# Two-layer decoder trunk on one core: both heads of a pair on the two halves of the array

## The reference, cut to what matters

```python
scores = jnp.einsum('bdnqhc,bdnkhc->bdnhqk', qs, kk) * (hd ** -0.5)
scores = jnp.where(allowed[:, None], scores + bias, NEG_INF)
m = jnp.max(scores, axis=-1)
p = jnp.exp(scores - m[..., None])
l = jnp.sum(p, axis=-1)
o = jnp.einsum('bdnhqk,bdnkhc->bdnqhc', p, vv.astype(jnp.float32))
...
cross = cross_attention(qc, mem_n, w_mem_kv[i])
x = x + jnp.concatenate([mix, cross], axis=-1) @ w_out[i]
```

## Time and profile before

| | us |
|---|---|
| median of 3 runs | 1661.31 |
| the profiled execution | 1662.92 |
| its span | 1661.1 |
| TensorE busy (PE) | 1584.7 (95%) |
| VectorE busy (DVE) | 1306.5 (79%) |
| ScalarE busy (ACT) | 1117.8 (67%) |
| GpSimd busy (POOL) | 79.8 (5%) |

### The profile page before, as it was taken

How to read it: one execution, slowest core, us unless ns; L and a number is a source line. 1 busy time by engine, 2 the same in 40 slices (tenths; PEclk the granted TensorE clock), 3 DMA queues, 4 the chain that set the end, 5 groups by cost and what they waited for, 6 DMA issues and landing times.

```text
span 1661.1 us, 25537 instructions
## 1 busy us (share of the span) xinstructions
PE 1584.7 (95%) x8450; PEld 1341.2 (81%) x8450; DVE 1306.5 (79%) x1687; ACT 1117.8 (67%) x1442; POOL 79.8 (5%) x57
## 2 busy tenths in 40 slices
PE   7899988999988989799999999999999999999996
PEld 6899966999987766688888888888888888888885
DVE  4777755555557763799899899899899899999996
ACT  5554445434443653687887878888878878878874
POOL 1422100000000000000000000000000000000000
PEclk9999988999998998799999999999999999999998
DMA  9744425566632235599999999999999999999992
GB/s 263 196 126 119 135 64 149 158 187 181 186 84 66 81 129 189 182 401 387 367 398 386 356 389 382 374 385 376 382 384 367 390 383 367 391 385 354 403 387 77
DMA packets 226976, 455.34 MB, mean 274 GB/s; under 512 B 12832, under 2 KB 120496, under 8 KB 226928
## 3 DMA queue, kind: packets, MB, share of 16 engines
q1 hardware_dynamic: 222784, 439.52, 72.9%
q0 software_dynamic: 4144, 15.22, 3.7%
HBM read 445.52 MB, written 9.18 MB: 274 GB/s over the span
## 4 chain that ended last, share of the span: by engine, by line
PE 90%; DVE 5%; ACT 2%; DMA 2%; issue 1%; DVEq 0%; POOL 0%; ACTq 0%; POOLq 0%
PE ps L664 27%; PE ps L665 26%; PE ps L666 26%; PE ps L737 2%; DMA big<-in_even_w_in 2%; PE ps L1029 1%; DVE w_lo L1345 1%; PE ps L759 1%; PE ps L735 1%; PE ps L746 1%; ACT w_hi L1065 1%; PE ps L691 1%; PE ps L763 0%; PE ps L971 0%; PE ps L962 0%
## 5 line engine op out<-in xcount | busy, mean ns | idle before, releaser
L1345 DVE TENSOR_TENSOR w_lo<-big,w_hi 128x1024 fp32r<-128x1024 f32 (+1 forms) x843 | 992.4, 1218 | 233.8 <-ACT w_hi L1065 157.0
L1286 ACT CAST w_hi<-big 128x1024 fp32r<-128x1024 f32 x672 | 693.8, 1056 | 138.0 <-PE ps L666 134.0
L664 PE MATMUL ps<-w_hi,m_hi 128*128 128x512 f32 (+1 forms) x1008 | 393.7, 391 | 4.6 <-DVE w_lo L1345 4.6
L665 PE MATMUL ps<-w_lo,m_hi 128*128 128x512 f32 (+1 forms) x1008 | 391.0, 388 | 0.0
L666 PE MATMUL ps<-w_hi,m_lo 128*128 128x512 f32 (+1 forms) x1008 | 390.6, 388 | 0.0
L664 PE MATMUL ps<-h_hi,w_hi 128*128 128x256 f32 (+1 forms) x824 | 240.5, 292 | 5.0 <-DVE w_lo L1345 5.0
L665 PE MATMUL ps<-h_lo,w_hi 128*128 128x256 f32 (+1 forms) x824 | 236.2, 287 | 0.0
L666 PE MATMUL ps<-h_hi,w_lo 128*128 128x256 f32 (+1 forms) x824 | 235.9, 286 | 0.0
L1065 ACT CAST w_hi<-big 128x1024 fp32r<-128x1024 f32 (+1 forms) x171 | 165.3, 977 | 95.5 <-PE ps L666 82.7
L664 PEld LDWEIGHTS ps<-w_hi,m_hi 128*128 128x128 f32 x1008 | 190.6, 189 | 44.7 <-issue 7.2
L666 PEld LDWEIGHTS ps<-w_hi,m_lo 128*128 128x128 f32 x1008 | 190.6, 189 | 38.7
(11 more groups left out here) (218 smaller groups left out, 1320.4 us busy)
## 6 DMA issues: line engine op xcount, KB each, us to landing
big<-in_odd_w_gate SPq DMA_DIRECT2D x112, 1024.0 KB, 7.3
big<-in_odd_w_up SPq DMA_DIRECT2D x112, 1024.0 KB, 7.5
big<-in_odd_w_down SPq DMA_DIRECT2D x112, 1024.0 KB, 7.4
big<-in_even_w_in SPq DMA_DIRECT2D x42, 512.0 KB, 4.2
big<-in_even_w_gate SPq DMA_DIRECT2D x22, 512.0 KB, 3.9
big<-in_even_w_up SPq DMA_DIRECT2D x22, 512.0 KB, 3.8
big<-in_even_w_down SPq DMA_DIRECT2D x22, 512.0 KB, 3.5
big<-in_w_out SPq DMA_DIRECT2D x20, 512.0 KB, 4.4
```

The source lines that it names most:

```text
L664: mm(dst, a[0], b[0], start=start, stop=False, **kw)
L665: mm(dst, a[0], b[1], start=False, stop=False, **kw)
L1286: nc.scalar.copy(w_hi[:, slot, :], ring[s][:, (u % 2) * UNIT:(u % 2 + 1) * UNIT]).then_inc(s_hi, 1)
L1345: return V.tensor_tensor(dst, src, lead.bitcast(F32), ALU.subtract)
```

## The change

The two heads of a pair now go through the scores together: `scores` issues their matmuls in turn, one on rows 0 to 63, one on rows 64 to 127, each into a bank of its own. `mix` does the same with the two column halves. For this the second head has buffers of its own: banks 1 and 7 and the second half of a projection bank for its scores (the third window's, of both heads), `zq` (where the indexer's queries and keys also live) for its scaled scores in layer 0, half of pr for its probabilities, `selm` or `zq` for their transpose. The orders of TensorE, ScalarE and VectorE in a step follow. Two semaphores are new: `third_left` (the first head's third window is written, before the second's is) and `third_read` (the next projection may take the bank). GpSimd's masks of a pair wait for the probabilities of both heads of the pair two before.

```diff
@@ buffers @@
-        qiT = sb("qiT", [P, 4, SEQ])
-        kiT = sb("kiT", [P, SEQ])
+        zq = sb("zq", [P, 5 * SEQ])
+        qiT = zq[:, 0:4 * SEQ].rearrange("p (c n) -> p c n", c=4)
+        kiT = zq[:, 4 * SEQ:5 * SEQ]
@@ views @@
-            return (z[:, o:o + pair.nbr * w].rearrange("p (b s) -> p b s", b=pair.nbr),
+            zs = zq if pair.nbr == NBR and hh else z
+            return (zs[:, o:o + pair.nbr * w].rearrange("p (b s) -> p b s", b=pair.nbr),
...
-        def score_banks(pair, hh, t):
+        def score_columns(pair, hh, t, b0, b1):
             if pair.nbr == 1:
                 n0 = SEQ if pair.cross else P
-                return ps[:, hh, (0, n0)[t]:(n0, n0 + SEQ)[t]].rearrange("p (b s) -> p b s", b=1)
-            if t == 0:
-                return ps[:, 0, 0:NBR * P].rearrange("p (b s) -> p b s", b=NBR)
-            return ps[:, 1:3, :].rearrange("p k n -> p (k n)")[:, 0:NBR * SEQ].rearrange("p (b s) -> p b s", b=NBR)
+                src = ps[:, hh, (0, n0)[t]:(n0, n0 + SEQ)[t]]
+            elif t == 0:
+                src = ps[:, hh, b0 * P:b1 * P]
+            elif b1 <= 2:
+                src = ps[:, (2, 7)[hh], b0 * SEQ:b1 * SEQ]
+            else:
+                src = ps[:, pair.bank(pair.nbr), hh * SEQ:(hh + 1) * SEQ]
+            return src.rearrange("p (b s) -> p b s", b=b1 - b0)
+        def value_bank(pair):
+            return ps[:, 5 if pair.l == 0 else 2, 0:SEQ]
+        def turned(pair, hh):
+            return ps[:, 5 if hh == 0 or pair.kind == "even" else 0 if pair.gs[-1] == NPAIR - 1 else 7, :]
+        def probs(pair, hh):
+            if pair.kind == "even":
+                return (pn[:, 0:CAUSAL], pr[:, 0:CAUSAL])[hh]
+            return pr[:, 512 * hh:512 * hh + (512 if pair.cross else CAUSAL)]
+        def probs_turned(pair, hh):
+            second = selm[:, :] if pair.kind == "even" else zq[:, 0:512]
+            return (pts[:, :], second)[hh]
@@ SyncE, before the load of the final gain @@
-            sp.wait_ge(s_isc, IDX_HEADS)
+            sp.wait_ge(s_at[1]["mixed"], 2 * NPAIR + 1)
@@ GpSimd, mask_pair @@
-                    pool.wait_ge(s_at[0]["scores_read"], 2 * g - 1)
+                    pool.wait_ge(s_at[0]["probs"], 2 * g - 2)
@@ TensorE, project @@
+                if pair.l == 0 and m == 0 and norm is None:
+                    pe.wait_ge(S["third_read"], PAIRS if pair.cross else pair.g)
@@ TensorE, scores @@
-                r = slice(HD * hh, HD * hh + HD)
                 k = keys(pair)
-                for b in range(pair.nbr):
-                    mm(score_banks(pair, hh, 0)[:, b, :], qT[r, pair.par, b, 0:P], k[r, 0:SEQ if pair.cross else P],
-                       start=True, stop=True)
-                    last = mm(score_banks(pair, hh, 1)[:, b, :], qT[r, pair.par, b, P:SEQ], k[r, :], start=True, stop=True)
-                last.then_inc(S["scores"], 1)
+                if pair.nbr == 1:
+                    turns = [[(0, 0), (1, 0)]] * 2
+                else:
+                    turns = [[(1, 2), (0, 0), (0, 1), (0, 2), (1, 0), (1, 1)], [(1, 0), (0, 0), (0, 1), (0, 2), (1, 1), (1, 2)]]
+                for i in range(len(turns[0])):
+                    for hh in range(2):
+                        t, b = turns[hh][i]
+                        r = slice(HD * hh, HD * hh + HD)
+                        if (hh, b) == (1, 2) and t:
+                            pe.wait_ge(S["third_left"], pair.g + 1)
+                        last = mm(score_columns(pair, hh, t, b, b + 1)[:, 0, :], qT[r, pair.par, b, tok(t)],
+                                  k[r, 0:SEQ if pair.cross or t else P], start=True, stop=True)
...
@@ TensorE, mix @@
+                for t in range(TT):
+                    for hh in range(2):
+                        h = slice(HD * hh, HD * hh + HD)
+                        n0 = 0 if pair.cross else P * t
+                        last = mm(ps[h, 6, n0:SEQ], v[:, t, h], probs_turned(pair, hh)[:, SEQ * t:SEQ * (t + 1) - n0],
+                                  start=(t == 0), stop=(t == TT - 1))
...
@@ TensorE, step (the two old orders are gone) @@
+                p(0)
                 if not now.cross:
                     turn_values(now)
...
+                p(1)
                 turn_probs(now, 0)
+                p(2, 3)
+                turn_probs(now, 1)
                 if nxt is not None:
+                    scores(nxt)
                 p(4)
+                mix(now)
@@ ScalarE, exps @@
+                if pair.kind == "even" and hh:
+                    act.wait_ge(S["summed"], 2 * pair.g + 1)
@@ ScalarE, step of layer 1 @@
-                    hi_mat(aft, 0)
-                    outs(hi, now, 0)
                     exps(now, 1)
                     e(0)
+                    values()
+                    outs(hi, now, 0)
                     probsT(now, 0)
-                    outs(hi, now, 1)
+                    hi_mat(aft, 0)
                     e(1)
                     e(2)
+                    probsT(now, 1)
+                    outs(hi, now, 1)
                     hi_mat(aft, 1)
                     hi_mat(aft, 2)
-                    probsT(now, 1)
@@ VectorE, head_scores (both heads in one call) @@
+                if pair.kind == "even":
                     dve.wait_ge(s_bm, NBR * pair.g + NBR)
+                    dve.wait_ge(S["scores"], 2 * pair.g + 2)
+                    read_scores(pair, 0, 1, 2, 3)
+                    read_scores(pair, 1, 1, 2, 3).then_inc(S["third_read"], 1)
+                for hh in range(2):
...
+                    read_scores(pair, hh, 0, 0, pair.nbr)
+                    read_scores(pair, hh, 1, 0, min(pair.nbr, 2)).then_inc(S["scores_read"], 1)
@@ VectorE, step @@
+                head_probs(now, 0)
                 if now.kind == "even":
-                    head_probs(now, 0)
-                    head_scores(now, 1)
                     lo_mat(aft, 0)
                     lo_mat(aft, 1)
                     head_probs(now, 1)
-                    for m in range(2, 5):
-                        lo_mat(aft, m)
+                    lo_mat(aft, 2)
+                    lo_mat(aft, 3)
                 else:
-                    head_scores(now, 1)
-                    head_probs(now, 0)
+                    head_probs(now, 1)
+                    outs(lo, now, 0)
                     lo_mat(aft, 0)
...
                 if nxt is not None:
-                    head_scores(nxt, 0)
+                    head_scores(nxt)
+                if now.kind == "even":
+                    lo_mat(aft, 4)
```

More of the change, by code:

```diff
@@ L717, in turn_values @@
                 for t in range(TT):
-                    last = tr(ps[:, 7, tok(t)], vT[:, tok(t)], ident)
+                    last = tr(value_bank(pair)[:, tok(t)], vT[:, tok(t)], ident)
                 last.then_inc(S["turned_v"], 1)
@@ L742, in turn_probs @@
                 pe.wait_ge(S["probs"], 2 * pair.g + hh + 1)
-                pe.wait_ge(S["probsT"], 2 * pair.g + hh + 1)
+                pe.wait_ge(S["probsT"], 2 * pair.g + 1 + (hh if pair.kind == "even" else 0))
+                if pair.kind == "even" and not hh:
+                    pe.wait_ge(S["values"], pair.g + 1)
                 for a, b in ([(0, 0), (1, 2), (2, 1), (3, 3)] if pair.cross else [(0, 0), (1, 1), (2, 2)]):
-                    last = tr(ps[:, 5, tok(b)], pn[:, tok(a)], ident)
+                    last = tr(turned(pair, hh)[:, tok(b)], probs(pair, hh)[:, tok(a)], ident)
@@ L829, in stream @@
                     pe.wait_ge(s_me, 2 * 2)
-                scores(first, 0)
+                scores(first)
                 steps(l, pe, step)
@@ L1124, in probsT @@
                 act.wait_ge(S["probs_turned"], 2 * pair.g + hh + 2)
-                act.wait_ge(S["mixed"], 2 * pair.g + hh + 1)
+                act.wait_ge(S["mixed"], 2 * pair.g + 1)
                 n = 512 if pair.cross else CAUSAL
-                nc.scalar.copy(pts[:, 0:n], ps[:, 5, 0:n]).then_inc(S["probsT"], 1)
+                nc.scalar.copy(probs_turned(pair, hh)[:, 0:n], turned(pair, hh)[:, 0:n]).then_inc(S["probsT"], 1)
             def step(now, nxt, aft):
@@ L1134, in e, with values @@
                         evac(nxt, m)
-                if not now.cross:
-                    act.wait_ge(S["turned_v"], now.g + 1)
-                    nc.scalar.copy(vN[:, :, :].rearrange("p t n -> p (t n)"), ps[:, 7, 0:SEQ]).then_inc(S["values"], 1)
+                def values():
+                    if not now.cross:
+                        act.wait_ge(S["turned_v"], now.g + 1)
+                        nc.scalar.copy(vN[:, :, :].rearrange("p t n -> p (t n)"), value_bank(now)).then_inc(S["values"], 1)
                 exps(now, 0)
@@ L1378, in norm_lo, with read_scores @@
                                 hi_[:, c, :]).then_inc(s_nlo, 1)
-            def head_scores(pair, hh):
+            def read_scores(pair, hh, t, b0, b1):
+                zv, pv, n0 = views(pair, hh)
```

(28 more changed lines are left out.)

83 lines of the change are left out of this document (30 added, 53 removed).

## The result

Four runs of the changed kernel beside four of the kernel before, on one chip: a median of **1609.36 us** (1608.71 to 1611.96) against 1660.46 (1655.68 to 1663.27), a ratio of 0.9698 with a 95% interval of 0.9673 to 0.9724. That is 51 us faster. The forecast was 1624 with a range of 1617 to 1640: the sign is right, the size is missed by 13 us, and the result lies outside the range. The profiled execution took 1611.96 us, 51.0 less than the one that the prediction was summed against.

What follows compares the result with a forecast made beforehand. TensorE was taken to bound layer 0's steps, hand-overs layer 1's. Terms −18.2 − 8.1 − 4.2 − 7.3 = −37.8 took the profiled 1662.92 us to 1625.1; the median being 1.6 lower, 1624 us, range 1617 to 1640.

Steps and rivals of the forecast that it cites:

- Part 1: Scores of both heads on the two row halves run at once: −2.16 us per layer-0 pair.
- Part 2: Both heads' products with the values on the two column halves overlap: 0.80 us saved per layer-0 pair.
- Rival one: Column halves do not overlap in the products with the values: +6.3 us, 1630 us; chance 0.18.
- Part 3: Scores right behind the second transpose wait for the kT copy: TensorE waits about 0.34 us per layer-0 step.
- Part 4: VectorE and GpSimd in layer 0 keep up with the later mask: step 18.95 us, −18.2 us over 7 steps.
- Rival two: VectorE closes the loop later, through the third mask operation or slower hand-overs: 1630 us; chance 0.15.
- Part 5: End of layer 0, pairs 7 to 9: fewer scores and mix blocks and 1.0 us less waiting, −8.1 us.
- Part 6: Layer 1: step closes at 8.9–9.0 us, −0.6 × 7 = −4.2; pairs 7 to 9 give −7.3.
- The clock rival: New TensorE gaps drop the granted clock to half over layer 1's steps and more: slower, 1671 us; chance 0.04.

Runs made afterwards that it cites:

- run 5: Changed kernel with all first-head score matmuls issued first and TensorE waiting for the last to finish before the second head's: 1641.98 us.
- run 6: Changed kernel with layer 0's fifth projection put between the two heads' products with the values: 1616.76 us.
- Run 7: Changed kernel with GpSimd's mask additions waiting only for the score reading of the pair two before, as in the kernel before: 1616.14 us.
- run 8: Kernel before with only the late mask: additions wait for both heads' probabilities of the pair two before: 1658.95 us, ratio 0.9993.
- run 9: Changed kernel with one ScalarE weight cast of layer 1 moved ahead of the second head's exponentials: 1605.84 us.
- run 3: Kernel before with useless transposes in two TensorE waits, at pair 7 of layer 0 and pair 8 of layer 1: 1658.94 us.
- run 4: Changed kernel with useless transposes in its three longest TensorE waits around the cross pairs: 1609.96 us.
- runs 13, 14: Changed kernel and kernel before, each with useless transposes only in the norms, indexer, router and start of the experts: 1603.3 and 1654.22 us.
- run 10: Changed kernel with useless transposes in TensorE's longest waits ahead of and at the start of the experts, cross pairs included: 1606.38 us.

## Why the prediction was right and where it failed

**Part 1 was right.** Both heads' scores take 2.17 us in the trace, and taking the overlap away (run 5) costs 2.27 a pair.

**Part 2 was right.** Both products take 0.80 us, and taking their overlap away (run 6) costs 0.73 a step. Rival one is out. The Trainium skill, SBUF — State Buffer (Who interferes with whom), gives TensorE a single read port for the moving operand. That doesn't make two column halves take turns here (0.80 us for both). The ratio from the Trainium skill, TensorE: Matmul & The Clock Gate (Measured speedup vs the span model), is for three tiles; two halves overlapped without loss.

**Part 3, small and a little short.** The scores start 0.70 us behind the second transposes (115.55 and 116.25), which take 0.25 themselves, so TensorE stood about 0.45 us; 0.34 was forecast. The prediction's words for it don't add up either: 0.04 and 0.37 less 0.3 make 0.1. The moved load of the final gain showed nowhere.

**Part 4, right.** Splits of 1.2 us beside GpSimd, nothing lost by the score reading (1.14 against 1.15), the step 18.87 for 19.0; the seven steps gave 19.1 us for 18.2. Run 7 shows that the later mask carries 6.8 us of the whole, run 8 that it does so only in the new order. One detail came out otherwise, by luck without harm: the forecast had two mask operations nearly through when the second split begins. Only one was, and the split lost nothing because it began 0.13 us ahead of the next. GpSimd's three operations take 5.57 us, hardly less than before (5.78); VectorE no longer loses the 2.0 us. Rival two (VectorE closes later) is out; the probabilities of the second head are ready 0.07 us ahead of their transposes, so it was near.

**Part 5 was right**: the end of layer 0 gave 8.3 us for 8.1.

**Part 6 failed**, in both of its terms. The first is the step: "That closes at 8.9–9.0", measured 8.62. From the first score reading to the end of the first head's scaling, 4.6 us where 4.9 were summed; transposes, copy, cast and splits 4.0 where 4.1 were. The likely reason, argued and not tested: a chain of some 15 short operations was summed from their mean durations, but their records overlap; two that follow one another on VectorE take 0.55 us as one row where each has 0.29 and 0.35. Six of the seven steps took 8.6 to 8.8 us and the last, from pair 6 to pair 7, only 7.97, which the flat "0.6 × 7" did not have: it was 9.58 before like the others. Why it fell more is not shown. Together the seven gave 3.2 us more than forecast, about 1 of them from that last step. The mechanism was right (run 9).

The second term is the end of layer 1: 5.8 for the blocks and "1.5 of waiting", 7.3 in all, measured 11.2. The waiting was not what it missed: TensorE's idle time there fell by 0.9 us. Its busy time fell by 10.4 where the blocks were priced at 5.8. The sum took all of the work at full clock and put the clock at nothing, while about 17 of the 38.4 us had been at half clock and only about 3 of 27.1 still were. The fills bear this out in part. In the kernel before, one (run 3) raised the clock there from 0.78 to 0.90 and took 2.7 us off (38.4 to 35.7), with about 7 us still at half clock; the changed kernel won 1.0 by its own (run 4, 27.1 to 26.1). So at least 1.7 of the 3.9 us are shown to be half clock. That the rest is too is likely from the busy times, but no run held the kernel before at full clock there. That the change would raise the clock there, the prediction neither said nor priced.

**Outside the attention** the prediction had zero, because the change touches nothing there. Of some 5 us, 2.3 lie between the layers and all but 0.6 of them go with the fills in both kernels. The 1.5 at the very start are within what it varies between traces of kernels that don't differ there: the first pair starts between 69.5 and 73.2 us in the traces of the 15 experiments. The 1.2 of the rest are small but may be real: without stage fills it takes 1016.4 to 1017.0 us in the traces of the old order and 1015.4 to 1016.2 in those of the new. What makes them is open.

**The clock rival** was priced on one side only, as a loss. The trace had the other side too: the earlier trace rows showed the clock at 0.50 in a stretch where TensorE was 84% busy, and a change that alters the waits there can move such a stretch, either way, as run 3's fill did. The range should have been open to that by 5 us below, and even then the steps of layer 1 would have put the result 2.6 us outside.

## What to carry to other kernels

Where both heads of a pair use half of the array each, put them next to each other: on this chip f32 matmuls on two row halves and on two column halves both run fully side by side, and each pair of blocks costs one. Before trusting an experiment that "undoes" such an overlap, look at the block in its trace: reordering the issue alone left half of one overlap and all of the other. Once the bound has fallen, look again at what used to be hidden: the mask's place was worth nothing before and 6.8 us after, and the place of one cast 3.5. And when a stretch of the kernel before ran at half clock, price its work at that clock, and say what the change does to it.

## What was not expected of the hardware

- TensorE takes matmuls of the second half from behind a queue of the first's: with all score passes of one head issued ahead, the other head's started after 1.2 us, and the block took 3.36 us in place of 2.17 alternating and 4.44 drained.
- Filling TensorE's waits with useless transposes raised the mean clock from 0.981 to 0.992 and gave 6 us (runs 13, 14), but a fill that starts when the clock is already at 1.2 GHz runs at that pace (4.95 us for 22) and delays the work behind it.
- Time at half clock cost little in most places: with all waits filled the changed kernel's mean clock rose from 0.981 to 0.993, by an estimate from these means some 39 us less at half clock, and its time fell by 3.0 us (run 10). At the end of layer 1 of the kernel before, 10 us less gave 2.7 (run 3). That other engines set the pace in the cheap stretches is a guess.
- Where a VectorE split and a GpSimd addition meet, the one that began first kept its time. A split begun ahead of the addition took 1.22 us, one begun under it 2.21; begun ahead both took 1.22 and 1.25, and the additions took 2.08 and 2.28 in place of 1.29.
